# Twenty-two conditioning slabs moved out of the dense channel mixer into the two normalisation stops around it

## What is computed

```
mod_x = (silu(c) @ w_ada[l] + b_ada[l])[:, None, :]
mod_c = silu(c_ctx) @ w_ada[l] + b_ada[l]
hx = modulate(rmsnorm(x, g_pre_mix[l]), sh1, sc1)
y_x, y_c = mixer_sublayer(hx, hc, ...)
x = x + gt1 * rmsnorm(y_x, g_post_mix[l])
hx = modulate(rmsnorm(x, g_pre_ffn[l]), sh2, sc2)
x = x + gt2 * rmsnorm(channel_mixer(hx, l, ...), g_post_ffn[l])
```

## Time and profile before

| | us |
|---|---|
| median of three runs | 2311.72 |
| lowest, highest | 2309.64, 2318.03 |
| the profiled execution, its own time | 2310.47 |
| its span in the trace | 2308.6 |
| mean granted clock of TensorE | 0.992 of full speed |

### The profile page before, as it was taken

One profiled execution on the slowest core, in us unless ns is written; L12 is line 12 of the kernel. 1 busy time (PEld: TensorE's weight loads), 2 busy tenths in 40 slices (PEclk: granted clock), 3 DMA queues, 4 the chain that ended last, 5 costly groups with the idle time before them and its releaser, 6 DMA issues.

```text
span 2308.6 us, 55953 instructions
## 1 busy us (share of the span) xinstructions
PE 2254.1 (98%) x24794; PEld 1654.6 (72%) x24794; DVE 751.7 (33%) x1563; ACT 558.5 (24%) x1090; POOL 49.9 (2%) x63
## 2 busy tenths in 40 slices
PE   7999999999999999998999999999999999999999
PEld 4777877778878887887888995555555555555556
DVE  4465354534633223366637651000000000101002
ACT  4345343423322222234535530000000000000001
POOL 0000010000200000000011000000000000000000
PEclk8999999999999999999999999999999999999999
DMA  6323232224754244213334479999999999999992
GB/s 256 122 110 129 82 147 109 96 115 182 228 194 167 105 164 160 95 55 110 110 103 139 165 302 395 394 407 381 407 382 411 380 408 378 414 376 411 394 418 108
DMA packets 86186, 548.96 MB, mean 238 GB/s; under 512 B 10256, under 2 KB 13456, under 8 KB 25936
## 3 DMA queue, kind: packets, MB, share of 16 engines
q1 hardware_dynamic: 52880, 352.68, 39.9%
q10 hardware_dynamic: 28912, 178.14, 19.6%
q0 software_dynamic: 4176, 14.81, 2.0%
HBM read 529.08 MB, written 16.52 MB: 236 GB/s over the span
## 4 chain that ended last, share of the span: by engine, by line
PE 87%; DVE 7%; ACT 3%; issue 2%; DMA 1%; ACTq 0%; DVEq 0%; SPq 0%
PE S L1807 17%; PE O L1807 13%; PE pp L1453 9%; PE pp L1455 8%; PE pp L1454 8%; PE T L1807 8%; PE S L1453 2%; DVE wsp L978 2%; PE S L1454 2%; PE S L1455 2%; PE T L1453 2%; PE T L1454 2%; PE T L1455 2%; PE pp L1512 2%; PE T L1608 1%
## 5 line engine op out<-in xcount | busy, mean ns | idle before, releaser
L1807 PE MATMUL S<-slabs,M 128*32 128x256 f32 x7168 | 470.1, 380 | 0.0
L978 DVE TENSOR_TENSOR wsp<-raw,wsp 128x1024 fp32r<-128x1024 f32 (+3 forms) x248 | 264.1, 1086 | 323.4 <-ACT wsp L635 322.2
L1807 PEld LDWEIGHTS S<-slabs,M 128*32 128x32 f32 x7168 | 227.7, 110 | 153.6 <-issue 8.6
L1453 PE MATMUL pp<-hx,wsp 128*128 128x512 f32 (+1 forms) x800 | 285.2, 356 | 20.2 <-DVE M L1196 4.7
L1807 PE MATMUL O<-slabs,M 128*32 128x256 f32 x5376 | 294.7, 379 | 0.0
L1408 DVE TENSOR_TENSOR M<-M,S 128x256 f32<-128x256 f32 x56 | 23.6, 422 | 800.2 <-ACT M L928 800.2
L1454 PE MATMUL pp<-hx,wsp 128*128 128x512 f32 (+1 forms) x800 | 277.4, 347 | 0.0
L1455 PE MATMUL pp<-hx,wsp 128*128 128x512 f32 (+1 forms) x800 | 277.2, 346 | 0.0
L1807 PE MATMUL T<-slabs,M 128*32 128x256 f32 x3584 | 275.4, 379 | 0.0
L1807 PEld LDWEIGHTS O<-slabs,M 128*32 128x32 f32 x5376 | 173.2, 110 | 114.9 <-issue 1.3
L635 ACT ACTIVATE wsp<-raw 128x1024 fp32r<-128x1024 f32 (+3 forms) x248 | 224.1, 935 | 28.4 <-PE pp L1455 19.7
(11 more groups left out here) (244 smaller groups left out, 2358.9 us busy)
## 6 DMA issues: line engine op xcount, KB each, us to landing
slabs<-in_w_moe SPq DMA_DIRECT2D x175, 1024.0 KB, 9.4
slabs<-in_w_moe ACTq DMA_DIRECT2D x161, 1024.0 KB, 9.6
raw<-in_w_main SPq DMA_DIRECT2D x84, 1024.0 KB, 5.0
M<-in_w_main SPq DMA_DIRECT2D x40, 1024.0 KB, 4.9
raw<-in_w_br SPq DMA_DIRECT2D x24, 512.0 KB, 3.6
xm<-in_w_main SPq DMA_DIRECT2D x8, 1024.0 KB, 4.9
raw<-in_w_dn SPq DMA_DIRECT2D x8, 768.0 KB, 4.2
moe_rows<-M POOLq DMA_DIRECT2D x14, 384.0 KB, 9.7
```

Of the source, the lines that this page charges most:

```text
L978: dve.tensor_tensor(wsp[:, slot, 1, 0:w], raw[:, rslot, half * w:half * w + w], wsp[:, slot, 0, 0:w], ALU.subtract).then_inc(lo_done, 1)
L1453: mm(dst, w_hi, x_hi, start=first, stop=False)
L1807: ins = mm(banks[g // 2][32 * c:32 * c + 32, 256 * (g % 2):256 * (g % 2) + 256], x(k, g), slab_e[i % RAW_E][:, 1024 * k + 256 * c:1024 * k ...
```

## The change

The 22 slabs leave the gate/up loops. Each stop takes eleven of them (`ADA_STOP`). `stop_product` is the same eight matmuls, but its weights are a window in `c_pad`, which has 30 zero columns ahead of the two vectors: slab n puts its two rows at columns 2n and 2n+1 of each group of 32, so that eleven products sum into the one bank O[0] without touching each other. One copy by ScalarE, one turn of 22 columns and two bias additions then serve all eleven. The products stand where `keep_up` stood: product 0 ahead of the first cast, 1 and 2 behind it, 3 to 10 behind the sums of blocks 0 to 7. Six and three idle matmuls stay behind the second cast, around the turn.

The slabs have buffers of their own, written by SP ahead of or in the stop. For the first stop, four are loaded once the mixer's first output tile is done, four when its last tile is done, and three when products 0, 1 and 2 have freed their buffers. For the second, six are loaded during the second half of the channel mixer, four when its last tile is done, one behind product 0. TensorE's wait ahead of each down stage is for the first half of the gated tiles only, the rest being waited for at the second part. The zero fill by GpSimd now waits until four tiles of the channel mixer are done. `sel` grows from 2 to 32 columns, `c32` becomes part of a padded tile of 8 x 62.

```diff
-        ada_f = [view(M, 2048 * j, 2048) for j in range(2)]
+        ada_m = [view(M, 2048 * j, 2048) for j in range(2)]
+        stop_buf = [ada_m + [slabs[:, n, :] for n in (4, 5, 0, 1, 2, 3)] + ada_m + [slabs[:, 4, :]],
+                    ada_m + [slabs[:, n, :] for n in (6, 7, 8, 9, 0, 1, 2, 3)] + [ada_m[0]]]
...
             for g in range(2, N_SLABS):
+                if g == g_gu[0]:
+                    for n in range(4):
+                        load_stop(0, n, step_of[0, "wout", 0]["t"])
+                if g == g_gu[0] + 2:
+                    for n in range(4, ADA_STOP):
+                        load_stop(0, n, t_stop[0] if n < 8 else t_stop[0] + n - 7)
...
+                if g == g_mix[1] + 2:
+                    for n in range(6, ADA_STOP):
+                        load_stop(1, n, t_stop[1] + n // 10)
                 load(g)
...
             pool.wait_ge(x_upd, 8)
+            pool.wait_ge(tile_done, t_gu[0] + 4)
...
                 norm_root(n, N)
-                act.wait_ge(mod_ready, (1, 2, 3, 3)[n // 2])
+                if n < 6:
+                    act.wait_ge(tile_done, t_stop[n // 4] + ADA_STOP)
+                    act.activation(adr_f[:, 0, :], O[0][:, 0:256], ACT.Copy).then_inc(stop_rows, 1)
+                act.wait_ge(mod_ready, (1, 2, 3, 4)[n // 2])
...
             prenorm(2, 0, 1, TOK)
+            stop_mods(0, pp[1])
+            for part in range(2):
+                own.link(am_part(1, part))
+            gate_bias(1)
             ffn()
...
+            def stop_product(b, n):
+
+                pe.wait_ge(stop_full[n], 16 * (b + 1))
+                for k in range(KT):
+                    r0 = 32 * (k % 4)
+                    ins = mm(O[0][r0:r0 + 32, 0:256], c_pad[:, k, 30 - 2 * n:62 - 2 * n], stop_buf[b][n][:, 256 * k:256 * k + 256],
+                             start=(n == 0 and k < 4), stop=(n == ADA_STOP - 1 and k >= 4))
+                ins.then_inc(tile_done, 1)
...
-                keep_up(5)
+                if n < 5:
+                    stop_product(n // 2, 0)
+                else:
+                    keep_up(5)
                 norm_cast(n, N)
...
-                if k == KT - 1:
-                    keep_up(5)
-                    norm_cast(n, N)
-                else:
-                    keep_up(3 if N == TOK else 1)
+
+            def stop(b, n):
+
+                stop_product(b, 1)
+                stop_product(b, 2)
+                for k in range(KT):
+                    norm_sum(n, k, TOK)
+                    stop_product(b, k + 3)
+                norm_cast(n, TOK)
+                keep_up(6)
+                if b == 0:
+                    pe.wait_ge(taken[1], step_of[0, "wout", KT - 1]["use"])
+                stop_turn(b, (pp[1], T[0])[b])
+                keep_up(3)
...
-                            if s == 1:
-                                turn(i, 0)
-                            elif not first:
-                                turn(i - 1, 1)
-                            pe.wait_ge(ada_full[s], ffn_full[s] + 8 * f0 + 16 + 16 * i)
-                            pe.wait_ge(taken[s], use_gu[h] + i)
-                            ada_product(pp[s], ada_f[s]).then_inc(tile_done, 1)
...
-                    turn(nF // 2 - 1, 1)
-                    pe.wait_ge(hF_done, f0 + nF)
+                    pe.wait_ge(hF_done, f0 + nF // 2)
```

More of the change, by code:

```diff
@@ L135 @@
 ADA_FIRST = 8
-ADA_FFN = sum(F_HALF)
-ADA_MIXER = [(0, s) for s in range(ADA_FIRST, ADA_SLABS)] + [(1, s) for s in range(ADA_SLABS - ADA_FFN)]
+ADA_STOP = 11
+ADA_MIXER = [(0, s) for s in range(ADA_FIRST, ADA_SLABS)] + [(1, s) for s in range(ADA_SLABS - 2 * ADA_STOP)]
 ADA_ORDER = [s for i in range(ADA_FIRST // 2) for s in (i, ADA_FIRST // 2 + i)]
@@ L275, in build_program @@
         ada_full, first_mod = [sem(f"ada_full{j}") for j in range(4)], sem("first_mod")
+        stop_full = [sem(f"stop_full{n}") for n in range(ADA_STOP)]
+        stop_rows = sem("stop_rows")
         hi_done, lo_done = sem("hi_done"), sem("lo_done")
@@ L642, in split_to, with stage_ahead @@
                     nxt[0] += 1
-            def stage_ahead(u0, gated, t0, w, i, s, last):
+            def stage_ahead(u0, t0, w, i, s, last):
                 if last and s == 1:
@@ L1485, in norm_cast, with stop_turn @@
                 ins.then_inc(cast_done, 1)
+            def stop_product(b, n):
[5 more added lines that the diff above has]
+                ins.then_inc(tile_done, 1)
+            def stop_turn(b, cols):
+                pe.wait_ge(stop_rows, b + 1)
+                for h in range(2):
+                    ins = mm(cols[:, 32 * h:32 * h + 2 * ADA_STOP], adr_f[:, 0, P * h:P * h + P], sel[:, 0:2 * ADA_STOP], start=True, stop=True)
+                ins.then_inc(cols_done, 1)
             def norm_sum_added(n, N):
@@ L1517, in ada_turn @@
                 for h in range(2):
-                    ins = mm(dst[:, bass.ds(col + 2 * h, 2)], rows[:, P * h:P * h + P], sel[:], start=True, stop=True)
+                    ins = mm(dst[:, bass.ds(col + 2 * h, 2)], rows[:, P * h:P * h + P], sel[:, 0:2], start=True, stop=True)
                 return ins
@@ L1748, in _ @@
             mixer(0, 1, 0)
-            keep_up(12)
-            for k in range(KT):
-                norm_sum(2, k, TOK)
-            keep_up(12)
+            stop(0, 2)
             ffn()
-            keep_up(12)
-            for k in range(KT):
-                norm_sum(4, k, TOK)
-            keep_up(12)
+            stop(1, 4)
             mixer(1, 5, 2)
@@ L1943, in _pack_dense @@
     dns, f = [], 0
+    for s in range(ADA_STOP):
+        ada(1, ADA_SLABS - 2 * ADA_STOP + s)
     for nF in F_HALF:
```

87 lines of the change are left out of this document (53 added, 34 removed).

## The result

The changed kernel takes **2300.04 us** (median of 7 runs, 2293.02 to 2302.79) against 2310.98 us for the kernel before, measured beside it: a ratio of **0.9941, 95% interval 0.9926 to 0.9957**. The forecast was 2282, its range 2274 to 2295. The profiled execution took 2300.04 us with a span of 2298.2; that is 10.4 us less than the earlier trace rows, where the working gave 29.4. The direction was right, the size a third of what was said, and the median lies outside the range. One of the runs reported further down (e12, 2526.99 us at a mean granted clock of 0.846) was a slow one and is left out of its ratio.

The account below looks back on a forecast made before the run. TensorE, busy 98% of the span, was taken as the bound. Channel mixer -34.9 and stops +5.5 gave -29.4 from 2310.5, so 2281.1; the runs' median lies 1.2 above, hence 2282 us, range 2274 to 2295.

Parts of the forecast that it names:

- Stops, the loop over blocks: Both stops: sum plus product takes 1.97 us per block, 0.39 more than before, over seven blocks each; 5.5 us added.
- Stops, the rest, at nothing: Stops outside the block loop: products 0, 1, 2 and 10 replace idle matmuls or cover waits; no cost.
- the clock falls in the stops: Rival: one-column sums and 32-column products drop both stops to 1.2 GHz, costing 5.5 + 38; 2320 us; 3%.
- The window 16 to 24 us: Prologue turning from sums to first products, at clock 1.00; cited against the rival that the clock falls in the stops.
- the 0.72 behind the channel mixer: Granted clock over 1001.78 to 1006.00, behind a TensorE wait and one-column sums; cited for the falling-clock rival.
- -8.1 for the block's price: Stops' block loop: lower bound, VectorE's 1.39 us setting the pace; used for the forecast's own range 2277 to 2288.
- The channel mixer: Gate/up loops and ends of halves: turns, products and waits leave, tiles 10.9 us apart; 34.9 us gained.
- The slabs: First stop's loads: no product waits, margin shrinking from 5 us to 1.7; late-slab rival 2295 us, 8%.
- The zero fill: Moved from the stop into the gate/up loop, costing nothing; rival that it delays weights, 2291 us, 5%.
- ScalarE's copy and VectorE's five small additions: Around the stops: copy precedes the later cast; additions fall in VectorE's 1.58 us wait, otherwise costing about 1 us.
- The block at a clock of 1.00: One stop block, a sum of eight matmul rows and a product, taken as 1.97 us.
- the estimate of 0.44 for the whole: One product as four rounds of 256 columns, near 0.44 us; set aside because the trace showed 0.93 to 1.07.

Follow-up runs that it names:

- e12: e11 with idle matmuls in the second stop behind the second and sixth blocks' products instead of the fourth's; 2291.11 us, ratio 0.9857 to the kernel before.
- e10: Kernel before without idle matmuls in the first seven blocks of both stops, nothing in their place; ratio 0.9998.
- e3: Kernel before, eight narrow matmuls with mostly zero weights replacing three idle matmuls in each of both stops' first seven blocks; 2333.83 us, ratio 1.0049.
- e4: As e3 on the kernel before, but all 32 weight columns carry numbers; 2332.01 us, ratio 1.0051.
- e14: As e4 on the kernel before, with sixteen narrow matmuls a block instead of eight; ratio 1.0069.
- e6: Kernel before with sixteen products' worth of narrow matmuls (mostly zero weights) in a row behind the first stop; ratio 1.0047.
- e7: Changed kernel plus five idle matmuls behind each stop's third product, behind the fourth block's product, and ahead of the channel mixer's last sums; 2289.49 us, ratio 0.9884.
- e11: As e7, but the second stop's first product and five idle matmuls exchange places; 2290.66 us, ratio 0.9858 to the kernel before.
- e15: As e11, with the stops' block products done two at a time behind every second sum; 2286.71 us, ratio 0.9869 to the kernel before.
- e5: Kernel before with four matmuls of 128 weight columns replacing the three idle matmuls in each of the first seven blocks of both stops; ratio 1.0061.
- e8: The changed kernel, not edited, run again beside e7 on the same chip; 2301.59 us, ratio 0.9931 to the kernel before.

## Why the prediction was wrong

**The step that failed** is "Stops, the loop over blocks", the term of 0.39 us a block and 5.5 us in all. It priced the three idle matmuls by the time they took, and the product that replaced them by the time it took, both at a clock of 1.00. The runs showed that the idle matmuls held that clock: without them (e10) both stops ran at 0.50, and with eight narrow matmuls in their place (e3, e4) three stops of four. The blocks measured 21.0 us where the term had 5.5, and "Stops, the rest, at nothing" measured 5.7, by the same low clock: 26.8 in all. It was there among the rivals, *the clock falls in the stops*, with the right mechanism and a chance of 3%.

Two readings made that chance too low. The window 16 to 24 us at 1.00 was taken for the same mix of work, "from sums to its first products". The trace of before has this in it:

```profile
18.72 1.93 PE L1512 MATMUL S<-M 128*32 128x256 f32 x32
20.58 1.18 PE L1518 MATMUL T<-sel,M 128*128 128x2 f32 x8
```

These are two products, 20.58 - 18.72 = 1.86 us, for each stretch of light matmuls, where a block of the stop has one product of 1.0 us; the sums ahead of them are of 512 columns, not of one. That is the proportion of e14 (sixteen narrow matmuls to a sum), which held 1.00, and e6 shows that products in a row hold the clock by themselves. And the trace did have the warning, the 0.72 behind the channel mixer, which was put down in part to a wait; e10 shows one-column sums at 0.50 with hardly any wait.

The rival's own size was off the other way: 43.5 us for the two stops against 26.8. In the first stop the low level lasted from 588 to 615.3, some 27 us, of which about half is loss; in the second, but for a dip at 984 to 987 that the kernel before has as well (at 1004 to 1007), it began only at 998.

One sum of the working doesn't come out: with -8.1 for the block's price the forecast's own range would begin at 2274, not at 2277. Nothing hung on it.

**What held.** The channel mixer: 35.5 us measured, 34.9 set down, with tiles 10.88 apart, the down stage directly behind the last T matmul, and TensorE waiting once for VectorE's low parts at the second tile, for 0.85 us. The slabs: no product waited for one, though the loads issued there took a median of 10.2 us from issue to landing, and the two into `M` 13.5 (the rows below, of the DMA issues from 578 to 602 us). At half the clock the products came later than forecast, so this was no hard test; but in e7, at 1.00, none waited either. Its last slab was issued at 584.75 and took 15.2 us, and its product came at 601.72, 1.8 us later than it landed; the working had 1.7. The zero fill ran inside the gate/up stage, and no wait of TensorE came of it (its one wait for low parts, at 632.11, is ahead of the fill, which starts at 643). ScalarE's copy and VectorE's five small additions stayed hidden. The block at a clock of 1.00 took 1.98, where 1.97 was set down.

```profile
slabs<-in_w_main SPq DMA_DIRECT2D x5, 1024.0 KB, 10.2
M<-in_w_main SPq DMA_DIRECT2D x2, 1024.0 KB, 13.5
```

**Not foreseen.** The kernel before has a dip at the start of the second mixer that is absent after (windows of before, then after, where the same work comes 8.6 us sooner):

```profile
1046.00:1048.00 2.00, 2.00 (x11) 2.00 (x11) 0.00 (x0) 0.00 (x0) 0.00 (x0) 0.50 0.71 291
```

```profile
1038.00:1040.00 2.00, 2.00 (x19) 2.00 (x19) 0.00 (x0) 1.01 (x2) 0.00 (x0) 1.00 0.34 143
```

Between TensorE's waits on either side of it lie 1053.83 - 1044.45 = 9.38 us before and 1043.70 - 1035.81 = 7.89 after: 1.5 of the 2.1 us gained there. Why it is absent was not tested; e11 and e15 have it again, so it may be luck.

**The two pages.** On a change of tiling mode, the Trainium skill's "TensorEngine Tiling (Array Packing)", "Key Properties", agrees in kind: a product between sums takes 0.99 to 1.00 us, in a row 14.02 / 16 = 0.88. On column groups that run at once (the Trainium skill's "TensorE: Matmul & The Clock Gate", "Part 3: Packing small matmuls — row/col tiling") the prediction said that the trace disagrees, and that was a wrong reading. Four wide fp32 matmuls of 256 columns take 590.74 - 588.92 = 1.82 us in e5, 0.45 each, so eight narrow ones in 0.88 us (e6) come out as two rounds of four at once. The rule agrees with these rows; the estimate of 0.44 for the whole was made with half the time that such an fp32 matmul needs.

## What to carry to other kernels

An idle matmul has two prices: the time it takes, and the clock it holds for its neighbours; before it is replaced by useful work, ask of each neighbour whether it would keep the clock alone. Where light work (here one-column sums) is spread through a stretch, two groups of five dense matmuls a stop (e7, e15) did nearly what seven groups of three had done. And when the clock is in part chance, look at the mean granted clock of every execution, of the kernel compared with too, before a ratio is read. And a window that is cited for the clock has to contain the same mix in the same order, not merely the same instructions.

## What the hardware showed that I had not expected

TensorE can be busy for 100% of a stretch and be granted half its clock: 588 to 603 us of sums in e10, 588 to 614 in the changed kernel. Whether a given stretch falls is in part chance: the same first stop dipped in e12 and not in e11, the same eight narrow fillers lost the clock in e3's first stop and kept it in its second, and the kernel before itself comes in two groups of times. The time of a kernel follows it from run to run: e8's seven runs go from 2291.90 us at a mean granted clock of 0.988 to 2311.98 at 0.978, while e7's five stay within 2286.91 to 2291.98 at 0.990 to 0.993. Holding the clock buys not only time but a steadier one.
